# Interchanging the inner loops of three matmul helpers, so that successive matmuls go to different accumulators

## What is computed

```
h   = rms_norm(x) * gain
p   = h @ w_in                     # 2048 -> 5376 columns: attention q, k, v; recurrence q, f, i, g
A   = sliding-window attention (16 heads, 2 key/value heads, width 64, window 128)
B   = gated linear recurrence (8 heads of width 128)
x   = x + concat(A, B) @ w_out     # 2048 -> 2048
h   = rms_norm(x) * gain
u   = causal_conv3(h @ w_up)       # 2048 -> 11264
x   = x + (silu(u[:, :5632]) * u[:, 5632:]) @ w_down   # 5632 -> 2048
```

## Time and profile before

| | |
|---|---|
| median of three runs | 1169.47 us (1169.41 to 1169.59) |
| span of the profiled execution, first to last instruction | 1167.6 us |
| TensorE matmuls | 6924, busy 1153.6 us (99% of the span) |
| TensorE weight loads | 6924, busy 1018.1 us (87%) |
| VectorE, ScalarE | busy 790.0 us (68%), 588.5 us (50%) |
| DMA | 204.16 MB, 175 GB/s over the span |

### The profile page before, as it was taken

How to read it: one execution, slowest core, us unless ns; L and a number is a source line. 1 busy time by engine, 2 the same in 40 slices (tenths; PEclk the granted TensorE clock), 3 DMA queues, 4 the chain that set the end, 5 groups by cost and what they waited for, 6 DMA issues and landing times.

```text
span 1167.6 us, 19529 instructions
## 1 busy us (share of the span) xinstructions
PE 1153.6 (99%) x6924; PEld 1018.1 (87%) x6924; DVE 790.0 (68%) x1187; ACT 588.5 (50%) x832; POOL 6.3 (1%) x33
## 2 busy tenths in 40 slices
PE   6999999999999999999999999999999999999998
PEld 5999999999988888888888888888888888888886
DVE  6856778685855557787777877878878744444442
ACT  7566736363634455555555555555545433333332
POOL 2000000000000000000000000000000000000000
PEclk9999999999999999999999999999999999999999
DMA  7543445454545655656566666666665656666562
GB/s 229 178 123 92 127 146 165 141 162 129 170 135 181 184 175 185 194 183 195 184 193 189 188 190 187 189 189 191 186 195 183 192 186 189 207 186 205 186 209 78
DMA packets 171996, 204.16 MB, mean 175 GB/s; under 512 B 6438, under 2 KB 139959, under 8 KB 171703
## 3 DMA queue, kind: packets, MB, share of 16 engines
q1 hardware_dynamic: 170854, 201.57, 56.3%
q10 hardware_dynamic: 1104, 2.10, 0.5%
HBM read 201.54 MB, written 2.10 MB: 174 GB/s over the span
## 4 chain that ended last, share of the span: by engine, by line
PE 98%; DVE 1%; DMA 1%; ACT 0%; issue 0%; SPq 0%
PE bank L1161 28%; PE bank L1162 14%; PE bank L1192 10%; PE bank L1191 10%; PE bank L1193 10%; PE bank L1175 7%; PE bank L1178 7%; PE bank L1177 7%; PE bank L1329 2%; PE bank L1129 1%; DMA xt<-in_x_dram 1%; PE bank L1262 0%; DVE hs L714 0%; PE bank L1237 0%; PE bank L1331 0%; PE bank L1236 0%
## 5 line engine op out<-in xcount | busy, mean ns | idle before, releaser
L694 DVE TENSOR_TENSOR w_lo<-raw,w_hi 128x1024 fp32r<-128x1024 f32 x380 | 463.4, 1222 | 305.8 <-ACT w_hi L395 304.7
L395 ACT CAST w_hi<-raw 128x1024 fp32r<-128x1024 f32 x380 | 398.6, 1052 | 488.9 <-PE bank L1193 189.2
L1161 PE MATMUL bank<-hs,w_hi 128*128 128x512 f32 x1408 | 488.9, 394 | 0.2 <-DVE hs L714 0.2
L1162 PE MATMUL bank<-hs,w_lo 128*128 128x256 f32 x1408 | 390.2, 277 | 0.0
L1161 PEld LDWEIGHTS bank<-hs,w_hi 128*128 128x128 f32 x1408 | 264.0, 188 | 61.7 <-DVE hs L714 0.5
L1162 PEld LDWEIGHTS bank<-hs,w_lo 128*128 128x128 f32 x1408 | 264.4, 188 | 0.1
L1175 PE MATMUL bank<-hs,w_hi 128*128 128x256 f32 x672 | 196.0, 292 | 0.5 <-DVE w_lo L694 0.5
L1178 PE MATMUL bank<-hs,w_lo 128*128 128x256 f32 x672 | 190.0, 283 | 0.0
L1177 PE MATMUL bank<-hs,w_hi 128*128 128x256 f32 x672 | 189.9, 283 | 0.0
L1191 PE MATMUL bank<-w_hi,gated 128*128 128x512 f32 x352 | 139.2, 396 | 0.0
L1192 PE MATMUL bank<-w_lo,gated 128*128 128x512 f32 x352 | 139.2, 396 | 0.0
(11 more groups left out here) (177 smaller groups left out, 792.3 us busy)
## 6 DMA issues: line engine op xcount, KB each, us to landing
raw<-in_w_ffn_up_dram SPq DMA_DIRECT2D x176, 512.0 KB, 3.6
raw<-in_w_ffn_down_dram SPq DMA_DIRECT2D x88, 512.0 KB, 4.5
raw<-in_w_in_dram SPq DMA_DIRECT2D x84, 512.0 KB, 3.8
raw<-in_w_out_dram SPq DMA_DIRECT2D x32, 512.0 KB, 4.0
xt<-in_x_dram SPq DMA_DIRECT2D x2, 1024.0 KB, 5.9
out_dram<-xt ACTq DMA_DIRECT2D x3, 512.0 KB, 7.0
out_dram<-xt ACTq DMA_DIRECT2D x2, 256.0 KB, 2.5
rows<-in_ffn_conv_w_dram SPq DMA_DIRECT2D x3, 44.0 KB
```

What stands on the lines that cost most here:

```text
L395: act.copy(w_hi[:, i, :], raw[:, i, :]).then_inc(units_hi, 1)
L694: dve.tensor_tensor(w_lo[:, i, :], raw[:, i, :], w_hi[:, i, :].bitcast(F32), ALU.subtract)\
L1161: pe.matmul(banks[b][:, :], w_hi[:, i, c], x_k, start=(i == 0 and k == 0), stop=False)
L1162: last = pe.matmul(banks[b][:, 0:SEQ], w_lo[:, i, c], x_k[:, 0:SEQ], start=False, stop=(i == RING - 1 and k == 3))
```

## The change

In `unit_channels` the two matmuls of each (k, b) become two loops over b: first the 512-column matmul of `w_hi` for both banks, then the 256-column matmul of `w_lo` for both. In `unit_w_in` each of the three products is done for both halves of the bank before the next. In `unit_tokens` the loop over t becomes the innermost, except in the units with `signal_first_tile`, which keep their order. Each matmul has the operands and the output that it had, the `start` and `stop` flags follow the first and the last matmul of an output, and the waits and the signals stand where they stood.

```diff
 # unit_channels
                 for k in range(4):
+                    x_k = hs[:, 4 * i + k, :]
+                    c = [slice(k * GC + b * P, k * GC + (b + 1) * P) for b in range(2)]
                     for b in range(2):
-                        c = slice(k * GC + b * P, k * GC + (b + 1) * P)
-                        x_k = hs[:, 4 * i + k, :]
-                        pe.matmul(banks[b][:, :], w_hi[:, i, c], x_k, start=(i == 0 and k == 0), stop=False)
-                        last = pe.matmul(banks[b][:, 0:SEQ], w_lo[:, i, c], x_k[:, 0:SEQ], start=False,
+                        pe.matmul(banks[b][:, :], w_hi[:, i, c[b]], x_k, start=(i == 0 and k == 0), stop=False)
+                    for b in range(2):
+                        last = pe.matmul(banks[b][:, 0:SEQ], w_lo[:, i, c[b]], x_k[:, 0:SEQ], start=False,
                                          stop=(i == RING - 1 and k == 3))
 # unit_w_in
+                    c = [slice(k * GC + b * P, k * GC + (b + 1) * P) for b in range(2)]
+                    o = [dst[:, b * SEQ:(b + 1) * SEQ] for b in range(2)]
                     for b in range(2):
-                        pe.matmul(o, w_hi[:, i, c], x_hi, start=(i == 0 and k == 0 and b == 0), stop=False,
+                        pe.matmul(o[b], w_hi[:, i, c[b]], x_hi, start=(i == 0 and k == 0 and b == 0), stop=False,
                                   skip_group_check=True)
-                        pe.matmul(o, w_hi[:, i, c], x_lo, start=False, stop=False, skip_group_check=True)
-                        last = pe.matmul(o, w_lo[:, i, c], x_hi, start=False,
+                    for b in range(2):
+                        pe.matmul(o[b], w_hi[:, i, c[b]], x_lo, start=False, stop=False, skip_group_check=True)
+                    for b in range(2):
+                        last = pe.matmul(o[b], w_lo[:, i, c[b]], x_hi, start=False,
                                          stop=(i == RING - 1 and k == 3), skip_group_check=True)
 # unit_tokens
+                def product(t, k, which):
+                    hi, lo = w_hi[:, i, k * GT:(k + 1) * GT], w_lo[:, i, k * GT:(k + 1) * GT]
+                    x_hi = src[:, k0 + k, t * P:(t + 1) * P]
+                    x_lo = src[:, k0 + k, SEQ + t * P:SEQ + (t + 1) * P]
+                    x_of, w_of = ((x_hi, hi), (x_hi, lo), (x_lo, hi))[which]
+                    return pe.matmul(banks[t][:, :], x_of, w_of, start=(k0 + k == 0 and which == 0),
+                                     stop=(which == 2 and k0 + k == k_all - 1))
...
+                if signal_first_tile:
+                    for t in range(TT):
+                        for k in range(2):
+                            for which in range(3):
+                                last = product(t, k, which)
+                        if t == 0:
+                            last.then_inc(first_tile_done, 1)
+                else:
                     for k in range(2):
+                        for which in range(3):
+                            for t in range(TT):
+                                last = product(t, k, which)
```

More of the change, by code:

```diff
@@ L1170, in unit_w_in @@
                     x_hi, x_lo = hs[:, 4 * i + k, 0:SEQ], hs[:, 4 * i + k, SEQ:2 * SEQ]
+                    c = [slice(k * GC + b * P, k * GC + (b + 1) * P) for b in range(2)]
+                    o = [dst[:, b * SEQ:(b + 1) * SEQ] for b in range(2)]
                     for b in range(2):
-                        c = slice(k * GC + b * P, k * GC + (b + 1) * P)
-                        o = dst[:, b * SEQ:(b + 1) * SEQ]
-                        pe.matmul(o, w_hi[:, i, c], x_hi, start=(i == 0 and k == 0 and b == 0), stop=False,
+                        pe.matmul(o[b], w_hi[:, i, c[b]], x_hi, start=(i == 0 and k == 0 and b == 0), stop=False,
                                   skip_group_check=True)
-                        pe.matmul(o, w_hi[:, i, c], x_lo, start=False, stop=False, skip_group_check=True)
-                        last = pe.matmul(o, w_lo[:, i, c], x_hi, start=False,
+                    for b in range(2):
+                        pe.matmul(o[b], w_hi[:, i, c[b]], x_lo, start=False, stop=False, skip_group_check=True)
+                    for b in range(2):
+                        last = pe.matmul(o[b], w_lo[:, i, c[b]], x_hi, start=False,
                                          stop=(i == RING - 1 and k == 3), skip_group_check=True)
@@ L1185, in unit_tokens @@
                 banks = pair_of(group)
-                for t in range(TT):
-                    for k in range(2):
[L1188 to L1195, removed]
+                def product(t, k, which):
[13 more added lines that the diff above has]
+                else:
+                    for k in range(2):
+                        for which in range(3):
+                            for t in range(TT):
+                                last = product(t, k, which)
                 last.then_inc(units_used, 1)
```

## The result

| | median | runs |
|---|---|---|
| before | 1169.53 us | 20 (1169.28 to 1170.62) |
| after | 1171.64 us | 20 (1171.52 to 1172.58) |

The ratio is 1.0018, with a 95% interval of 1.0011 to 1.0025. The profiled executions have spans of 1167.6 and 1169.7 us, so the whole difference lies inside the traces.

The account below looks back on a forecast made before the run. The prediction took TensorE's distances between matmul starts as the bound. Span 1167.6 + 0 (`unit_tokens`) + 0 (`unit_w_in`) + 4.7 (`unit_channels`) = 1172.3 us, plus 1.9 us from span to median, gave 1174.2 us; range 1158 to 1179 us.

Parts of the forecast that it names:

- TensorE alone bounds the kernel, and only the distances count: Whole kernel: TensorE busy 1153.6 of 1167.6 us, hardly waiting; the change matters only through distances between successive matmul starts.
- `unit_tokens`: 0: Down projection: changing the bank after each 512-column matmul gains nothing; 0 us, bounds 14 us either way.
- `unit_w_in`: 0: Input projection: alternating halves of one bank among 2016 256-column matmuls changes nothing; 0 us, bounds about 6 us either way.
- fills the distance: Input projection: the weight load occupies the time between matmul starts, so no order of outputs makes it shorter.
- `unit_channels`: 699.9 ns a k step, 4.7 us: Up projection: a k step of four matmuls grows from 693.2 to 699.9 ns, 4.7 us more over 704 steps.
- gave each kind of neighbourhood a fixed price: Up projection: mixed pair 346.6 ns, 512 to 512 233.3 ns, 256 to 256 120.0 ns, whatever else the stream does.
- all of its 6.7 ns: Up projection: loss per k step, because one 256-column matmul loses its advantage of standing beside a 512-column one.
- rival D: All three helpers settle in another rhythm, a few ns either way, -6 us in input projection alone; chance 0.04 upward, 0.08 downward.
- Rival A: Up projection: alternating banks removes a stall, giving 1160.0 us, or 1152 us if `unit_tokens` gains too; chance 0.20.
- Rival B: Whole kernel: average matmul cost depends on size and helper, not order, so time stays 1169.5 us; chance 0.28.

Follow-up runs that it names:

- b_others_only: Kernel before with only the new orders of `unit_w_in` and `unit_tokens`, `unit_channels` untouched: 1169.54 us, ratio 1.0 (0.9991 to 1.0009).
- a: Kernel before with only `unit_channels` in the new order: 1171.74 us, ratio 1.002 (1.0011 to 1.003).
- c: Kernel before, `unit_channels` only: sizes 512, 512, 256, 256 as in the change, but two bank changes a k step: 1171.70 us, ratio 1.0018.
- f_runs_of_eight: Kernel before, `unit_channels` only: in each unit eight 512-column matmuls, then eight of 256 columns: 1172.77 us, ratio 1.0028.
- d3: Kernel before, but in `unit_channels` the first and last k step of each group of 16 are 512, 512, 256, 256: 1178.23 us, ratio 1.0074.
- d2: Kernel before, `unit_channels` only: sizes still alternate, but in the 14 middle k steps of 16 the bank changes behind 512 columns: 1169.58 us, ratio 0.9999.
- i: Kernel before, but in `unit_channels` only the first k step of each group of 16 is 512, 512, 256, 256: 1173.84 us, ratio 1.0037.
- g: Kernel before, order kept, but both blocks of the up projection add into one bank (output not the reference's): 1169.49 us, ratio 0.9999.
- e: Kernel before, `unit_channels` only: per two k steps four 512-column matmuls, then four of 256 columns: 1175.21 us, ratio 1.0047.

## Why the prediction was right, and where its step was wrong

The direction and the place of the loss came as forecast; 1171.64 us lies in the range, 2.6 us under the value given. The mechanism was another, so that the right direction was luck.

- **TensorE alone bounds the kernel, and only the distances count.** Right. Counts, waits and the chain are the same; the 2.13 us are all distances in the up projection.
- **`unit_tokens`: 0.** Right. 944 matmuls in 220 us in both kernels; b_others_only shows the same on the clock.
- **`unit_w_in`: 0.** Right. 252 in 30 us in both. The remark that the weight load "fills the distance" does not follow from the earlier trace rows: the load's record is 0.19 us long and its matmul starts 0.11 us after the load did. What sets 120 ns is not shown.
- **`unit_channels`: 699.9 ns a k step, 4.7 us.** The term was mis-sized: it measured 696.7 ns and 2.1 us. The step that failed is the one that gave each kind of neighbourhood a fixed price, and above all the price of 256 columns beside 256, 120.0 ns, borrowed from the input projection. The changed kernel has all four kinds. Views of its timeline that begin between two equal neighbours show the second of them by itself:

```profile
599.98 0.39 PE L1161 MATMUL bank<-hs,w_hi 128*128 128x512 f32 x1
...
600.22 0.40 PE L1163 MATMUL bank<-hs,w_lo 128*128 128x256 f32 x2
...
600.33 0.28 PE L1163 MATMUL bank<-hs,w_lo 128*128 128x256 f32 x1
...
600.45 0.63 PE L1161 MATMUL bank<-hs,w_hi 128*128 128x512 f32 x2
```

With the start at 599.75 these are 0.23, 0.24, 0.11 and 0.12 us. Averaged over all starts from 460 to 900 us of the two traces, in ns:

| from, to | forecast | before | after |
|---|---|---|---|
| 512 to 512 | 233.3 | none | 232.9 |
| 256 to 256 | 120.0 | none | 114.6 |
| 512 to 256 | | 231.7 | 233.3 |
| 256 to 512 | | 115.0 | 115.8 |
| the last two together | 346.6 | 346.7 | 349.1 |

The price borrowed for 512 columns held (232.9 ns). Over 704 steps the 256-column price was 3.8 us too high, and the mixed pair, taken over unchanged, 1.8 us too low. Of the 3.3 ns a step that were lost, 2.8 ns lie behind the 512-column matmuls and 0.4 ns behind the 256-column ones (rounded), where the prediction had put all of its 6.7 ns. The loss is real (a and c repeat it), but an advantage of 256 columns beside 512 was not what was lost. In f_runs_of_eight 512 columns beside 512 even come down to 227 ns.
- **What the loss is instead.** The new order has a rhythm of its own, 696.7 ns a step. d3 against d2 shows that the rate of one and the same order depends on what disturbed the stream before (353.3 against 346.7 ns a pair); i shows that the state is kept for a whole group and changed by the next break. This comes nearest to rival D, to which the prediction gave 0.12 in all, 0.04 of it upward; but D expected it in all three helpers, and two kept their rates. The prediction had the evidence for it and used it only as a bound.
- **Rival A, alternating banks relieves a stall.** Refuted for this kernel: with the sizes in turn, no change of bank (g) and two a step in either position (before, d2) give 1169.5 to 1169.6 us; in the new order two (c) and four (a) give 1171.7 us.
- **Rival B, no change.** Not so: the interval of the ratio, 1.0011 to 1.0025, leaves out 1.

Still open: what in the chip makes these rhythms, why the new order settles at 696.7 ns, and why long runs of 512 columns settle at 227 ns with tokens moving and at 233.3 ns with weights moving. No run here separates the roles of the weight load's source and the moving operand's.

## What to carry to other kernels

Where an engine runs at 98% of the chain, read its rate as the time of many instructions (a count in a long stretch), then look whether the same order has more than one rate anywhere in the trace; if it has, the order is a state that can be lost, and a price per instruction taken from one place does not hold in another. A price borrowed from another helper with the same shape can be off by more than the effect at stake: 120.0 ns for 114.6 ns alone was 3.8 us here, beside a loss of 2.1 us. Alternating PSUM banks between successive accumulating matmuls bought nothing in this kernel, in which each matmul has a weight load and the reader of a bank waits for the end of the group anyway.

## What was not expected of the hardware

The steady rates are few and sharp: 120.0 and 233.3 ns for single sizes in two helpers, 346.7 or 353.3 ns for a pair of 512 and 256 columns, 696.7 ns for two and two. The averages hold to within 1 ns over tens of units, while single distances vary by several ns (112 to 118 ns behind 256 columns in the kernel before). All of these rates are close to multiples of 6.67 ns (18, 35, 52 and 53 times, and 209 times for two k steps of the new order); so are the units of e and f, 2806.7 and 2793.3 ns (421 and 419 times). No run here gives the reason. In i_one_break a single step of four matmuls in another order, once in 64, leaves its own group at 11.10 us or makes it 11.30 us, depending only on the rhythm that the stream was in; a single added matmul takes nothing but its own 0.12 us.
